# Every fourth weight remainder of two MLPs made by an accumulating transfer

## The reference

```python
def squared_relu_mlp(h, w_up, w_down):      # w_up 2048 x 8192, w_down 8192 x 2048
    a = jnp.square(jax.nn.relu(h @ w_up))
    return a @ w_down
...
for layer in range(DEPTH):
    h = rmsnorm(x, ln_mix_g[layer])
    x = x + mixer(h)
    h = rmsnorm(x, ln_mlp_g[layer])
    x = x + squared_relu_mlp(h, mlp_w_up[layer], mlp_w_down[layer])
```

## Time and profile before

| | us |
|---|---|
| median of 3 runs | 2117.44 (2116.82 to 2118.59) |
| the profiled execution | 2117.51 |
| its span, first to last instruction | 2115.8 |
| TensorE busy | 2095.8 (99%), granted clock 0.999 |
| VectorE busy | 1191.5 (56%) |
| ScalarE busy | 996.4 (47%) |
| GpSimd busy | 85.7 (4%) |
| weight loads (SyncE's queue) | 54.2% of 16 DMA engines, 380 MB |
| rounding, L586 | 754.0, x724, mean 1043 ns |
| remainder, L869 | 882.7, x724, mean 1224 ns |

### The profile page before, as it was taken

One profiled execution on the slowest core, in us unless ns is written; L12 is line 12 of the kernel. 1 busy time (PEld: TensorE's weight loads), 2 busy tenths in 40 slices (PEclk: granted clock), 3 DMA queues, 4 the chain that ended last, 5 costly groups with the idle time before them and its releaser, 6 DMA issues.

```text
span 2115.8 us, 26852 instructions
## 1 busy us (share of the span) xinstructions
PE 2095.8 (99%) x10506; PEld 1774.4 (84%) x10506; DVE 1191.5 (56%) x1429; ACT 996.4 (47%) x1417; POOL 85.7 (4%) x133
## 2 busy tenths in 40 slices
PE   8999999999999999999999999999999999999999
PEld 6887888888888888888888898888888888888887
DVE  5545555565555545655556687556555555554654
ACT  5555555444344434434445576444434434443442
POOL 0000000000000000000000255000000000000000
PEclk9999999999999999999999999999999999999999
DMA  7544554555555556555555533455555555555553
GB/s 250 186 145 161 168 167 140 181 177 199 199 185 194 191 190 196 182 197 179 199 187 180 155 124 121 160 182 178 201 195 190 188 199 187 192 194 187 179 201 135
DMA packets 198445, 381.99 MB, mean 181 GB/s; under 512 B 10860, under 2 KB 17080, under 8 KB 198328
## 3 DMA queue, kind: packets, MB, share of 16 engines
q1 hardware_dynamic: 198280, 380.29, 54.2%
q10 hardware_dynamic: 48, 0.02, 0.0%
HBM read 378.19 MB, written 2.10 MB: 180 GB/s over the span
## 4 chain that ended last, share of the span: by engine, by line
PE 97%; DVE 1%; ACT 1%; DMA 1%; SPq 0%; issue 0%; POOL 0%; DVEq 0%; ACTq 0%; POOLq 0%
PE psum L1274 23%; PE psum L1223 19%; PE psum L1225 19%; PE psum L1224 19%; PE psum L1277 11%; PE psum L1338 1%; PE psum L1419 1%; DMA raw<-in_sf_w_in 1%; PE psum L1292 0%; DVE halves L869 0%; PE psum L1401 0%; PE psum L1247 0%; PE psum L1420 0%; PE psum L1385 0%; PE psum L1386 0%
## 5 line engine op out<-in xcount | busy, mean ns | idle before, releaser
L869 DVE TENSOR_TENSOR halves<-raw,halves 128x1024 fp32r<-128x1024 f32 (+1 forms) x724 | 882.7, 1224 | 753.9 <-ACT halves L586 753.1
L586 ACT CAST halves<-raw 128x1024 fp32r<-128x1024 f32 (+1 forms) x724 | 754.0, 1043 | 930.1 <-PE psum L1225 620.0
L1274 PE MATMUL psum<-h,halves 128*128 128x512 f32 x2048 | 639.1, 395 | 0.0
L1223 PE MATMUL psum<-halves,a 128*128 128x512 f32 x1340 | 525.4, 392 | 0.0
L1225 PE MATMUL psum<-halves,a 128*128 128x512 f32 x1340 | 521.8, 389 | 0.0
L1224 PE MATMUL psum<-halves,a 128*128 128x512 f32 x1340 | 521.5, 389 | 0.0
L1277 PEld LDWEIGHTS psum<-h,halves 128*128 128x128 f32 x2048 | 380.1, 188 | 87.7
L1277 PE MATMUL psum<-h,halves 128*128 128x256 f32 x2048 | 397.9, 278 | 0.0
L1274 PEld LDWEIGHTS psum<-h,halves 128*128 128x128 f32 x2048 | 314.2, 189 | 3.1 <-DVE halves L869 0.4
L1225 PEld LDWEIGHTS psum<-halves,a 128*128 128x128 f32 x1340 | 251.5, 188 | 52.9
L1223 PEld LDWEIGHTS psum<-halves,a 128*128 128x128 f32 x1340 | 251.6, 188 | 51.7 <-ACT nat L652 0.4
(11 more groups left out here) (187 smaller groups left out, 870.6 us busy)
## 6 DMA issues: line engine op xcount, KB each, us to landing
raw<-in_mlp_w_up SPq DMA_DIRECT2D x128, 1024.0 KB, 5.5
raw<-in_mlp_w_down SPq DMA_DIRECT2D x128, 1024.0 KB, 5.0
raw<-in_sf_w_in SPq DMA_DIRECT2D x47, 1024.0 KB, 5.1
raw<-in_sf_w_o SPq DMA_DIRECT2D x16, 1024.0 KB, 5.0
raw<-in_mla_w_o SPq DMA_DIRECT2D x16, 1024.0 KB, 5.0
raw<-in_mla_w_down SPq DMA_DIRECT2D x8, 1024.0 KB, 5.1
raw<-in_mla_w_ukv SPq DMA_DIRECT2D x8, 1024.0 KB, 5.1
raw<-in_mla_w_uq SPq DMA_DIRECT2D x8, 768.0 KB, 4.6
```

The lines of the kernel that those rows point to most:

```text
L586: nc.scalar.copy(half_piece(n, 0), raw_piece(n)).then_inc(hi_done, 1)
L869: v.tensor_tensor(half_piece(n, 1), raw_piece(n), half_piece(n, 0).bitcast(F32), ALU.subtract)\
L1223: mm(bank, x_hi, hi[:, i], start=(k == 0), stop=False)
L1274: last = mm(bank, half_piece(n, 0)[:, cols], src[:, k].rearrange("p s t -> p (s t)"), start=(k == 0), stop=(k == KT - 1))
```

## The change

In both MLPs the pieces with (n - start) % 4 == 3 take another way, 64 in each MLP, 128 in all. ScalarE, right after it has rounded such a piece, also writes the negated raw piece, rounded, where the remainder belongs: halves[..., 1] = round(-w) = -hi. It increments `negated`. GpSimd waits for that and issues a transfer SBUF to SBUF that adds the raw piece onto it: -hi + w = lo, 128 partitions x 4 KB. Its landing increments `acc_done`. VectorE skips the piece, and `lo_done` now counts only the other pieces. TensorE waits for both counts before such a piece. SyncE frees a raw slot whose last piece is such a one on `acc_done`. Its MLP loop is written out, block by block. GpSimd issues the 64 transfers of layer 0 between the decay factors and its layer-1 tasks, and the 64 of layer 1 behind those tasks.

```diff
+def by_dma(n):
+    for start in (P_MLP0, P_MLP1):
+        if start <= n < start + MLP_PIECES:
+            return (n - start) % 4 == 3
+    return False
+def acc_no(n):
+    return sum(by_dma(m) for m in range(n + 1))
+def lo_no(n):
+    return n + 1 - acc_no(n)
+ACC_BLOCK = 16
...
-            def free_slot(load, extra=0):
+            def free_slot(load):
                 if load >= SLOTS:
-                    sp_.wait_ge(lo_done, 2 * load - 2 * SLOTS + 2 + 2 * extra)
-                    if not isinstance(extra, int):
-                        sp_.nop()
+                    last = 2 * load - 2 * SLOTS + 1
+                    if by_dma(last):
+                        sp_.wait_ge(acc_done, 16 * acc_no(last))
+                    sp_.wait_ge(lo_done, lo_no(last))
...
+            def remainders(layer):
+                for i in range(NB * ACC_BLOCK):
+                        n = (P_MLP0, P_MLP1)[layer] + 4 * i + 3
+                        pool.wait_ge(negated, NB * ACC_BLOCK * layer + i + 1)
+                        pool.dma_start(half_piece(n, 1).bitcast(F32), raw_piece(n), accum_op=ALU.add).then_inc(acc_done, 16)
+            remainders(0)
             pool.wait_ge(rope_ready, 1)
...
             for n in (28, 29):
                 split_out(n)
+            remainders(1)
...
                 nc.scalar.copy(half_piece(n, 0), raw_piece(n)).then_inc(hi_done, 1)
+                if by_dma(n):
+                    nc.scalar.activation(half_piece(n, 1), raw_piece(n), ACT.Copy, scale=-1.0).then_inc(negated, 1)
...
             def split_lo(n, extra=0):
+                if by_dma(n):
+                    return
                 dve.wait_ge(hi_done, n + 1 + extra)
...
+            def halves_ready(n, blk):
+                pe.wait_ge(lo_done, lo_no(n) + (64 - ACC_BLOCK) * blk)
+                if by_dma(n):
+                    pe.wait_ge(acc_done, 16 * acc_no(n) + 16 * ACC_BLOCK * blk)
...
-                        pe.wait_ge(lo_done, n + 1 + 64 * blk)
+                        halves_ready(n, blk)
```

More of the change, by code:

```diff
@@ L339, in build @@
         hi_done, lo_done = sem("hi_done"), sem("lo_done")
+        negated, acc_done = sem("negated"), sem("acc_done")
         pieces_used = sem("pieces_used")
@@ L446, in mlp, with block @@
                 w_up, w_down = mlp_w_up[layer], mlp_w_down[layer]
-                with sp_.Fori(0, NB) as b:
+                def block(b0):
                     for c in range(8):
                         for l in range(4):
-                            load = load0 + 4 * c + l
-                            free_slot(load, 32 * b)
+                            load = load0 + 32 * b0 + 4 * c + l
+                            free_slot(load)
                             dst = raw[:, load % SLOTS].rearrange("p (k n) -> p k n", k=4)
                             if c < 4:
-                                src = w_up[4 * P * l:4 * P * (l + 1), bass.ds(b * D + c * N, N)]
+                                src = w_up[4 * P * l:4 * P * (l + 1), b0 * D + c * N:b0 * D + (c + 1) * N]
                             else:
-                                src = w_down[bass.ds(b * D + 4 * P * l, 4 * P), (c - 4) * N:(c - 3) * N]
+                                src = w_down[b0 * D + 4 * P * l:b0 * D + 4 * P * (l + 1), (c - 4) * N:(c - 3) * N]
                             sp_.dma_start(dst, src.rearrange("(k p) n -> p k n", p=P))\
                                .then_inc(raw_loaded[load % SLOTS], 16)
+                for b0 in range(NB):
+                    block(b0)
             def load_x(s):
@@ L1441, in mixer @@
                         kts, _ = shape_of(n)
-                        pe.wait_ge(lo_done, n + 1)
+                        pe.wait_ge(lo_done, lo_no(n))
                         if kind == "cols":
```

## The result

The changed kernel takes 2129.49 us (median of 4 runs, 2128.63 to 2129.94) against 2117.18 us for the kernel before, measured beside it: a ratio of 1.0056, 95% interval 1.0041 to 1.0071. It is slower, by 12.3 us; the forecast was slower by 61.

What follows compares the result with a forecast made beforehand. The prediction took TensorE to bound the kernel and summed the transfers' lateness over four margins, 19.0 + 7.2 + 24.7 + 9.9 = 60.9 us, onto 2117.5 us: 2178.4 us, 2.9% slower, range 2114 to 2345 us.

Steps and rivals of the forecast that it cites:

- What bounds the kernel: Whole kernel and both MLPs: TensorE, busy 99% with 97% of the chain; relieving VectorE is worth at most 0.4 us.
- The margins: Time from negation's end until TensorE wants the piece: 5.86 us down, 6.02 up, 5.17 late, 4.96 late and down.
- L: Time from the negation's end to the accumulating transfer's landing: 6.2 us, from 5.0 plus 1.2 for sharing; ends 2.7 and 7.5.
- ScalarE: In the MLPs it gains 128 negations of 1.05 us, 134 us, all within its idle time or waits: cost nothing.
- TensorE's second wait: An extra wait before each of 128 pieces, hidden because TensorE's queue is ahead: taken as 0, 6.5 us without cover.
- SyncE: Raw slots freed on the transfer's landing: costs nothing until landing takes 10.4 us; two loads then go out together.
- the late pieces: Pieces rounded behind ScalarE's copy of a chunk's right half: 24 charged 24.7 us, 8 wanted in the down half 9.9.
- the upper bound of 7.5: Longest landing in the forecast's case, from a 0.5 MB transfer behind others: 227.3 us of lateness, 2344.8 us.
- It fits: Rival: transfers land under about 5.26 us, within the margins, so no change, 2117.5 us; chance 0.35.
- Much longer: Rival: transfers take over 7.5 us to land, 2345 us and more; chance 0.15.
- Faster: Rival: VectorE's relief reaches TensorE, worth 0.4 us, 2117.1 us; chance 0.03 for over 0.2%.
- loads starved: Rival: raw slots freed so late that ScalarE waits for loads, from a landing of 10.4 us, 2716 us; chance 0.03.

Runs made afterwards that it cites:

- The run with VectorE's addition: Changed kernel, but VectorE adds the raw piece onto the negated half and GpSimd issues no transfer: 2117.88 us against 2117.6 before, ratio 1.0002.
- the spare-buffer run: Changed kernel, but negations and 128 accumulating transfers go onto a spare buffer and VectorE makes every remainder: 2117.05 us against 2117.6 before, ratio 0.9998.
- the run with twice as many: Changed kernel, but every odd piece goes the new way, 256 transfers: 2407.86 us against 2115.12 before (single runs).
- the plain copy: Changed kernel with a plain transfer in place of the accumulating one, so the product differs: 2122.53 us against 2115.12 before (single runs).
- the later transfers: Changed kernel with a GpSimd memset ahead of each of the second MLP's 64 transfers: 2139.03 us against 2115.12 before (single runs).
- the other pieces of the four: Changed kernel with (n - start) % 4 == 1 in place of 3: 2124.85 us against 2117.6 before, ratio 1.0034.

## Why the prediction was right or wrong

*What bounds the kernel.* Right: TensorE carries 95% of the chain, and the 149 us taken from VectorE gave nothing. The windows and pieces kept their pace.

*The margins.* Right. In the changed kernel a piece's first matmul starts 5.95 (down), 6.15 (up), 5.26 (late) and 5.06 us (late, down) behind the negation's end, in the median. It starts 0.04 to 0.13 us behind the landing at the earliest, so that the margins are 5.91, 6.01, 5.12 and 4.97, where the prediction had 5.86, 6.02, 5.17 and 4.96. What exceeds them moves everything behind by that much and 0.1 us: 6.5 us summed from 128 pairs of L and margin, 6.4 found in the first matmuls' shift, 7.8 with the matmuls behind them.

*ScalarE.* Right, in the ordinary case and in the late one. The late negation in its timeline, with the squares' wait behind it:

```profile
977.95 1.02 ACT L816 COPY nat<-psum 128x1024 f32<-128x1024 f32 x1 [1.68 <-PE psum L1315]
978.86 1.05 ACT L618 CAST halves<-raw 128x1024 fp32r<-128x1024 f32 x1
979.81 1.06 ACT L620 ACTIVATE halves<-raw 128x1024 fp32r<-128x1024 f32 x1
981.52 1.05 ACT L866 CAST a<-nat 128x1024 fp32r<-128x1024 f32 x1 [0.65 <-DVE nat L1201]
```

From the copy's start to the last cast it is 3.57 us, as in the earlier trace rows: the negation filled what had been a wait. The run with VectorE's addition confirms it at 1.0002.

*TensorE's second wait.* Right at 0, by the same run.

*SyncE.* Right that two loads go out together, and that they cost nothing of their own (the spare-buffer run, 0.9998).

*L: this step failed.* The prediction had L = 5.0 + 1.2 = 6.2 us for each of 128 transfers. The 5.0 was the row of a 1 MB load, chosen because 1 MB has to be read; the transfer alone took 4.5 from issue, 4.8 with GpSimd's lag. The 1.2 was added to each, on the ground that loads fill most of the time; it is 0.24 in the median (5.04 - 4.80) and over 1.2 in 16 of the 128. Since the next pair of loads goes out only when the transfer has landed, the change itself keeps the two apart; an arriving transfer isn't thrown onto the traffic of before at random. The shortest margins go with the shortest L: the late pieces, which made 34.6 of the 60.9 us, find the pair gone (4.5 from issue in the rows above, L at most 5.58), and the wait falls on ordinary ones behind them. With 19 of 128 over their margin the term is 6.5 us and not 60.9.

*What the sum lacked.* Nearly half of the 12.3 us had no term: the back edges, 2.3 us, the half clock after the longest wait, 1.7, and the 0.1 behind each late landing, 1.4. At the end the last load and three stores go out one behind the other (2095.11 to 2100.61) and meet the transfer of 2101.47; the prediction priced that piece like the others. Its L of 7.92 lies over the upper bound of 7.5, the landing time of the first of these stores before.

*The rivals.* "It fits" named L under 5.26, and the median is 5.04. But it took one L for all, as I did, and a tail of 19 is what makes the loss. By one L of 5.04 its sum would have been 0.6 us. "Much longer" became real in the run with twice as many. "Faster" and "loads starved" found nothing: no rounding of the MLPs waits for a load.

On the Trainium skill: the plain copy took 2.9 us, close to the 3.2 of "DMA: Bandwidth & Descriptors" (Anatomy of one DMA), and the accumulating one 4.5, close to the 4.4 that I had worked out with the second source read of "Collectives: The Full Stack" (the section on the bandwidth ceiling). In the trace a 4 KB packet takes 339 ns accumulating and 160 ns copying, which fits two reads at twice the time and nothing for the addition. I had set this aside since the loads of the trace were slower than the fit; but those loads come from the chip's memory and this transfer never leaves SBUF. Whether that is the difference, no run shows. As the price of a transfer alone the estimate was better than my row; as the only L it would have had no piece late.

*What stays open.* That the loss at the loop's end is the branch is shown by writing the loop out, and the shorter lead of the changed kernel by the landings. Why the branch takes 4.1 to 6.3 us in every run with a loss there isn't shown. It isn't only that pieces come by transfer: with the same transfers on a spare buffer it took 3.8 us, without a loss, and 4.1, with 0.5. The first 16 KB packet of the instruction queue begins 1.0 to 1.2 us behind the branch's begin where nothing depends on a transfer, and with 64 of them; in the changed kernel and its other variants with a loop it begins 1.8 to 3.9 us behind. What delays it wasn't found. Nor was the 0.1 us behind each late piece.

## What to carry to other kernels

Before costing a transfer that others wait for, write down the margin of each use and the distribution of the landing, not one number for each: the loss is the part that sticks out, and half the transfers cost nothing where twice as many cost 290 us. Ask also what the new wait does to the traffic that it meets; here the loads were tied to its landing and moved out of its way, except at the end of the program, where the last loads and stores pile up. And if the bound engine gains nothing from the relief, the best case of such a change is no change: no version tried here beat the kernel before.

## What was not expected of the hardware

- An accumulating transfer of 0.5 MB inside SBUF takes 4.5 us from issue and its issue holds GpSimd for 0.86 us; a plain copy takes 2.8 to 2.9 and 0.53.
- A jump back in TensorE's loop takes its queue 3.4 to 3.8 us where nothing is lost, up to 6.3 in the runs with 128 transfers; the next matmul starts 0.26 us behind its end. It is free only while the queue is that far ahead, and a landing shortly before the use of the loop's last piece shortens the lead.
- TensorE's granted clock fell to about half for 3 to 4 us after waits of 1.95 us (the changed kernel), 2.44 us (the plain copy) and 2.52 us (the later transfers), and stayed at 1.00 after those of 1.8 and 1.6 us (the other pieces of the four). It cost another 1.7 us in the changed kernel, nearly as much as the wait, and 1.5 in the plain copy.
